# Three chunks of the third small slot moved from the trailing part of the second down half into its first three groups

## What is computed

```python
def _moe(h, w_router, w_up, w_down):
    ...
    top_val, top_idx = lax.top_k(logits, TOP_K)            # TOP_K = 2
    top_w = jax.nn.softmax(top_val, axis=-1)
    gates = jnp.sum(jax.nn.one_hot(top_idx, N_EXPERTS) * top_w[..., None], axis=1)
    out = jnp.zeros_like(hf)
    for e in range(N_EXPERTS):                             # 8 experts, EXPERT_FF = 3584
        out = out + gates[:, e:e + 1] * _swiglu(hf, w_up[e], w_down[e])
```

## Time and profile before

| | |
|---|---|
| median of 3 runs | 1822.9 us |
| lowest, highest | 1817.6, 1824.27 us |
| the profiled execution: its own time | 1818.49 us |
| its span, first to last instruction | 1816.6 us |
| PE (TensorE matmul) busy | 1696.3 us, 93% |
| DVE busy, ACT busy | 802.8 us (44%), 660.5 us (36%) |
| mean HBM rate over the span | 265 GB/s |
| mean granted TensorE clock | 0.979 |

### The profile page before, as it was taken

How to read it: one execution, slowest core, us unless ns; L and a number is a source line. 1 busy time by engine, 2 the same in 40 slices (tenths; PEclk the granted TensorE clock), 3 DMA queues, 4 the chain that set the end, 5 groups by cost and what they waited for, 6 DMA issues and landing times.

```text
span 1816.6 us, 24747 instructions
## 1 busy us (share of the span) xinstructions
PE 1696.3 (93%) x9694; PEld 1200.1 (66%) x9694; DVE 802.8 (44%) x1261; ACT 660.5 (36%) x946; POOL 31.3 (2%) x50
## 2 busy tenths in 40 slices
PE   5999989899999999999879999998999999998897
PEld 3885568788888778876666566565565565655564
DVE  2434655443223356735654333334442434333455
ACT  2325662422223235225733333332334333333241
POOL 1200000000000000000010000000000000000000
PEclk8999999999999999999989999999999999999999
DMA  9825753223322644220049999999999999999996
GB/s 345 202 93 199 289 188 114 70 93 120 108 85 93 253 153 140 93 93 24 33 183 420 421 420 421 421 420 389 414 362 422 403 411 421 420 421 385 415 378 274
DMA packets 112050, 481.85 MB, mean 265 GB/s; under 512 B 8218, under 2 KB 46280, under 8 KB 62784
## 3 DMA queue, kind: packets, MB, share of 16 engines
q1 hardware_dynamic: 109344, 472.66, 66.1%
q0 software_dynamic: 2592, 7.62, 1.9%
HBM read 477.38 MB, written 2.87 MB: 264 GB/s over the span
## 4 chain that ended last, share of the span: by engine, by line
PE 73%; DVE 10%; DMA 9%; ACT 4%; issue 3%; SPq 0%; DVEq 0%; ACTq 0%
PE PS L848 19%; PE PS L850 18%; PE PS L849 18%; DMA RAWB<-in_w_exp_up 5%; PE PS L1454 4%; PE PS L1527 3%; PE PS L875 2%; DMA RAWB<-in_w_exp_down 2%; DVE RAWAL L2757 2%; PE PS L1124 2%; ACT BH L2006 1%; PE PS L1146 1%; PE PS L1134 1%; ACT S L1780 1%; DVE RAWBL L2757 1%
## 5 line engine op out<-in xcount | busy, mean ns | idle before, releaser
L2133 DVE TENSOR_TENSOR WL<-RAW,WH 128x2048 fp32r<-128x2048 f32 (+1 forms) x61 | 137.6, 2256 | 290.3 <-ACT WH L1653 290.1
L848 PE MATMUL PS<-HH,WH 128*128 128x512 f32 (+1 forms) x600 | 228.2, 380 | 10.2 <-DVE HL L2172 3.0
L850 PE MATMUL PS<-HH,WL 128*128 128x512 f32 (+1 forms) x600 | 225.0, 375 | 0.0
L849 PE MATMUL PS<-HL,WH 128*128 128x512 f32 (+1 forms) x600 | 224.8, 375 | 0.0
L1653 ACT ACTIVATE WH<-RAW 128x2048 fp32r<-128x2048 f32 (+1 forms) x61 | 115.1, 1888 | 287.0 <-PE PS L850 287.0
L848 PE MATMUL PS<-BH,HE 128*128 128x512 f32 x448 | 181.8, 406 | 19.3 <-DVE RAWAL L2757 12.3
L2757 DVE TENSOR_TENSOR RAWBL<-RAWB,BH 128x2048 fp32r<-128x2048 f32 x42 | 96.3, 2293 | 201.0 <-ACT BH L2006 201.0
L850 PE MATMUL PS<-BH,LE 128*128 128x512 f32 x448 | 175.9, 393 | 0.0
L2006 ACT ACTIVATE BH<-RAWB 128x2048 fp32r<-128x2048 f32 x42 | 80.4, 1914 | 224.8 <-DMA RAWB<-in_w_exp_up 137.5
L2757 DVE TENSOR_TENSOR RAWAL<-RAWA,BH 128x2048 fp32r<-128x2048 f32 x41 | 93.9, 2290 | 144.8 <-ACT BH L2006 144.8
L848 PEld LDWEIGHTS PS<-BH,HE 128*128 128x128 f32 x448 | 84.4, 188 | 83.8 <-issue 30.2
(11 more groups left out here) (362 smaller groups left out, 2691.4 us busy)
## 6 DMA issues: line engine op xcount, KB each, us to landing
RAWA<-in_w_exp_up SPq DMA_DIRECT2D x112, 1024.0 KB, 10.3
RAWB<-in_w_exp_up SPq DMA_DIRECT2D x112, 1024.0 KB, 10.0
RAWA<-in_w_exp_down SPq DMA_DIRECT2D x56, 1024.0 KB, 9.7
RAWB<-in_w_exp_down SPq DMA_DIRECT2D x56, 1024.0 KB, 9.6
RAW<-in_w_mod SPq DMA_DIRECT2D x48, 1024.0 KB, 6.2
RAW<-in_w_ffn_up SPq DMA_DIRECT2D x22, 1024.0 KB, 5.0
RAW<-in_w_in_c SPq DMA_DIRECT2D x12, 1024.0 KB, 5.2
RAW<-in_w_ffn_down SPq DMA_DIRECT2D x10, 1024.0 KB, 5.2
```

Of the source, the lines that this page charges most:

```text
L848: mm(ps, ah, bh, start=start, stop=False)
L849: mm(ps, ah, bl, start=False, stop=False)
L850: return mm(ps, al, bh, start=False, stop=stop)
L2133: v.tensor_tensor(WL[:, c % 2, 0:n], raw("weight", c)[:, 0:n], WH[:, c % 2, 0:n].bitcast(F32), ALU.subtract).then_inc(s_lo, 1)
```

## The change

Group st of the second down half gets its chunk of small slot 2 right behind the big chunk when st < 3, as in the first half. Four chunks (st = 3 to 6) trail. Each of the four carries two gathers in `down(True)`. In `down(False)`, `scatter_last((0, 1))` now stands behind the second trailing chunk (st = 4) and `scatter_last((2, 3))` behind the third (st = 5). The table `order` is changed alike, so the SP queue loads in the new order, and from group 0 of the second half to its end chunks lie in other places of the ring. No instruction is added or removed on TensorE, ACT, DVE or POOL but for ACT's register instructions, and the same chunks are loaded.

```diff
@@ -209,8 +209,9 @@
         order += [(who, "d", st, 0) for st in range(NST) for who in (0, 1, "big", 2)]
-        order += [(who, "d", st, 1) for st in range(NST) for who in (0, "big", 1)]
-        order += [(2, "d", st, 1) for st in range(NST)]
+        WITH2 = 3
+        order += [(who, "d", st, 1) for st in range(NST) for who in (0, "big", 1, 2)[:4 if st < WITH2 else 3]]
+        order += [(2, "d", st, 1) for st in range(WITH2, NST)]
@@ -1590,26 +1591,28 @@
                             small_down(1, st, 0, more)
                             small_down(1, st, 1, more)
                             big_down(1, st)
+                            if st < WITH2:
+                                small_down(1, st, 2, more)
                             if st == 1:
                                 pe.wait_ge(s_back01, i + 1)
                                 pe.wait_ge(s_ylo, i * 10 + 5)
                                 scatter_half(0, 7, False)
                             if st == 2:
                                 scatter_half(1, 0, False)
-                        for st in range(NST):
+                        for st in range(WITH2, NST):
                             small_down(1, st, 2, more)
-                            if more and st < 4:
-                                if st == 0:
+                            if more and st < WITH2 + 4:
+                                if st == WITH2:
                                     pe.wait_ge(s_sel, i + 2)
                                     pe.wait_ge(s_selb, i + 2)
                                     pe.wait_ge(s_myd, i * 4 + 2)
-                                gather(i + 1, 2 * st)
-                                gather(i + 1, 2 * st + 1)
-                            if not more and st == 3:
+                                gather(i + 1, 2 * (st - WITH2))
+                                gather(i + 1, 2 * (st - WITH2) + 1)
+                            if not more and st == NST - 3:
                                 pe.wait_ge(s_myd, i * 4 + 1)
                                 pe.wait_ge(s_ylo, i * 10 + 7)
                                 scatter_last((0, 1))
-                            if not more and st == 5:
+                            if not more and st == NST - 2:
                                 pe.wait_ge(s_ylo, i * 10 + 9)
                                 scatter_last((2, 3))
```

## The result

| | before, same comparison | changed | difference |
|---|---|---|---|
| median of 14 runs each | 1819.55 us | 1826.53 us | +7.0 us |
| lowest to highest | 1815.66 to 1824.27 | 1822.33 to 1831.98 | |
| ratio | | 1.0041, 95% interval 1.0032 to 1.0051 | +7.5 us (+5.8 to +9.3) |
| profiled execution, its span | 1818.49, 1816.6 | 1826.15, 1824.3 | +7.7 |
| mean granted clock of that execution | 0.979 | 0.977 | |

The kernel is 0.4% slower, within the 0.5% that the prediction called no change. Forecast were +5.6 us and 1828.5, in a range from 1820.5 to 1834.5. The ratio's interval leaves no doubt of the sign. That 1828.5 lies only 2.0 us from the measured median is partly luck: it stood on a median of three runs, 1822.9, which is 3.3 us above that of 14, while the difference was forecast 1.4 us too small. On 1819.55 the same sum gives 1825.2.

The account below looks back on a forecast made before the run. TensorE was taken to bound the second down half, with the weight stream waiting for ring places. +2.8 us at the round change and +2.8 at the end, clock 0, gave +5.6 on 1822.9: 1828.5 us, range 1820.5 to 1834.5.

Parts of the forecast that it names:

- Step 1: Second down half: three small chunks move to where TensorE has no gap; its last big chunk ends 2.78 us later each round.
- The rival in which group 0 waits for data: Second down half: the 1.1 us margin fails and the stream paces group 0, 1.5 us a round: 1831.5; chance 0.07.
- Step 2: Round 0 to 1: last gather 2.78 us later, unshortened 7.75 us chain, TensorE idle about 5.0 us; cost +2.8 us.
- two waits end together: Before round 1's first big chunk's split: landing and ACT's work end together; only the landing comes earlier, gaining nothing.
- the lead of the stream is cut off by the ring: Round 1's up phase: ring waits, seen at 1410 to 1420, remove the stream's lead within one group.
- passes on in full: Round 1's up phase: the 2.8 us lateness from the round change stays whole; at the low end 0.9 is left.
- the bound that the prediction set against itself: Round 1's up phase: the prediction called itself wrong if that phase takes back more than 1.9 us.
- Step 3: Behind the last big chunk: tail keeps its length, two idle spots of about 1.3 us are hidden, starts 2.78 late: +2.8 us.
- Step 4: TensorE's clock behind the round-change gap and at the end: no extra loss taken, 0; at most 3.2 us more in each.
- The slower rival: Low clock through round 1's first big chunk and the closing scatters, 3.2 us each: +12.0 us, 1834.9; chance 0.13.
- The evened stream that gains: Second down halves: filling the weight stream where it starves gains 11.7 us, thus 1811.2; chance 0.05.
- Most given back at the round change: Round 0 to 1: only 0.9 of the 2.8 us passes on, 1826.6; chance 0.15.

Follow-up runs that it names:

- e3: The change with one small chunk moved in each round instead of three; ratio 1.0016 to the kernel before, median 1821.5 us.
- e4: The change with two small chunks moved in each round instead of three; ratio 1.0036 to the kernel before, median 1826.3 us.
- e8: The change with the moved chunk of groups 1 and 2 behind the scatter instead of ahead of it; 1827.1 us, one run.
- e5: Kernel before with gathers closer, six behind the third trailing chunk, and ACT's copy of small slot 2 after the split; ratio 1.0012 to the kernel before.
- e6: The change with gathers closer, six behind the second trailing chunk, and ACT's copy of small slot 2 after the split; ratio 1.0021 to the kernel before.
- e9: e5 with the first big up chunk loaded second in its group instead of fourth; ratio 1.0033 to the kernel before, median 1825.9 us.
- e10: Kernel before with only the first big up chunk loaded second instead of fourth in its group; ratio 1.0021 to the kernel before, median 1824.4 us.
- e2: Kernel before with three chunks moved in the last round's down phase alone; ratio 1.0021 to the kernel before, median 1822.4 us.
- e1: Kernel before with three chunks moved in round 0's down phase alone; ratio 1.0021 to the kernel before, median 1823.1 us.
- e7: The change with the two small sources scattered first at the end and the big ones after; ratio 1.0024 to the kernel before, median 1823.2 us.
- e11: The change with the edits of e6, e7 and e8 together; ratio 0.9998 to the kernel before, median 1818.3 us.
- e12: e11 with all eight gathers behind the first trailing chunk; ratio 0.9981 to the kernel before, median 1815.0 us.

## Why the prediction was right, and where not

**Step 1, three chunks at 2.78 us: right mechanism, mis-sized term.** The chunks do move from under a chain to a saturated TensorE, with no wait for data (chain of waits, and e3, e4). The rival in which group 0 waits for data is excluded: its +0.83 is the chunk's own time. The term that failed is the price of 0.93 each, taken from three chunks in one row. Joined to others one costs 0.83, beside the scatter 1.19, because it breaks a row of wide matmuls; 3.2 a round, not 2.78. e8 isolates the 0.35 of it.

**Step 2, the round change: right.** The chain stays (7.67 against 7.75), the idle time grows to 4.88 where about 5.0 was forecast, in two pieces where the text had one: 1.15 for ACT's FS ahead of the small up chunks, which it left out, and 3.73. That two waits end together was borne out by e5, e6, e9 and e10. That the lead of the stream is cut off by the ring shows in the 46 GB/s and in SP's wait of 10.5 us, but for another chunk than the prediction named: the first big chunk of round 1, which ends at 1392.7, and not one at 1410. That lateness "passes on in full" is nearly so. In the two profiled executions the up phase seems to give back 1.9 us (+5.0 to +3.2), just about the bound that the prediction set against itself. But that phase, from the end of its first big chunk, takes 272.5 us in the kernel before, 271.0 to 271.5 in e2, e5 and e10, where round 0 has no moved chunk, and 270.5 to 272.0 in the change, e1, e6 and e8. The kernel before was simply slow there in its profiled execution. At equal clock e1 keeps 2.4 of its 3.2, so up to 0.8 may be given back; runs that scatter by several us don't settle it.

**Step 3, the end: right.** Idle spots of 1.34 and 1.36 against "about 1.3", the tail unchanged, and e2 shows the last round's cost arriving whole at the end of the span. e7 shows what the tail hung on.

**Step 4, the clock at 0: the other term that was off.** The changed kernel's 14 runs have a mean granted clock of 0.9771 against 0.9783 in the 92 runs of the kernel before (for the 14 runs of it that stand beside the change, no clocks are known). By the slope of 0.97 us per 0.001 that is 1.1 us of the 7.0 to 7.5, give or take 0.7 (two standard errors), and 5.9 are left for the path, close to 2 x 3.2. e1, e5, the change and e7, all with 3.64 or 3.73 before the first big chunk, have 0.9771 to 0.9775, and e4 with 3.73 has 0.9766; before, e2, e6 and e11, with 2.45 to 2.56, have 0.9778 to 0.9783, and e12 with 1.70 has 0.9795. e9 and e10 don't fit this row (0.9773 and 0.9772 with 0.85 and 2.45; the kernel before had 0.9779 beside them), so the gap at the round change is a possible cause of the 1.1 us, not a shown one. The first big chunk speaks for half of it at most: the six profiles with 3.64 to 3.73 have it at 7.5 on average, the five with 2.45 to 2.56 at 7.0, and each group scatters by more than that (1.6 and 2.9 us). The kernel before and the changed one both show the fall (7.29 and 7.38). What else lowers the mean clock stays open. The slower rival (+12.0 by the clock) did not come, though a part of its mechanism may be, 1.1 of 6.4 us. By the rule of the Trainium skill, TensorE: Matmul & The Clock Gate, section Why this matters for your kernels, idle gaps between bursts of matmuls drop the clock; e1's 8.66 behind 3.73 agrees with it, e7's 5.76 behind 3.73 does not.

**The rivals.** The evened stream that gains is excluded: 411 instead of 383 GB/s and not a microsecond won from it. Most given back at the round change (0.9 left of 2.8) is excluded by e1: 3.8 by its ratio, 2.2 at the least by the interval, 2.4 at equal clock. The sum that fits is 3.2 + 3.2 for the path, less at most 0.8, and 1.1 for the clock: 6.7 to 7.5, against 5.6 forecast and 7.0 (medians) or 7.5 (ratio) measured.

## What to carry to other kernels

Before work is moved to where another resource has room, look whether the engine that does it has room there too. Small work under a chain that it does not set is free, and where its engine has no gap it costs its full time. When such work must leave its cover, refill the cover at once: put the gathers that start the chain earlier, and order the tail so that only what comes late stands last. What a moved instruction costs depends on its neighbours, so take its price from a row in the same surroundings.

## What was not expected of the hardware

- The first 128x512 matmul behind small down chunks takes 0.43 us in the chain where its followers take 0.23, and a small chunk that stands alone takes 1.00, where one more in a row of small ones adds 0.86. Splitting a row of like matmuls cost 0.35 us (e8 against the change).
- The same 24 matmuls behind the round change took 5.75, 7.29 or 8.66 us. A gap of 2.45 was followed by no fall in e2 and by one in the kernel before at 2.46; gaps of 3.73 by 5.76 (e7), 7.38 and 8.66 (e1). Whether the clock falls behind such a gap, and for how long, varies between executions; one profile shows one case of it.
- The mean granted clock goes with 42% of the variance of one kernel's times: 5.1 us between its five runs at 0.975 and its six at 0.981 (1822.3 and 1817.2). Cause and effect are not told apart by that.
